# Expert stages of a two-block transformer kernel: the gate factor moves from the closing addition to the eviction of each expert's rows

## What is computed

```python
gate = (p_group * top_p / sum(top_p)).reshape(m)      # two experts a token: m = 1024 rows
x_rows = xf[row_tok].reshape(n_blocks, 128, d)        # rows sorted by expert, in blocks of 128
def expert_block(xb, e):
    hcat = xb @ w13[e]                                # 1024 -> 2 x 512
    return (silu(hcat[:, :512]) * hcat[:, 512:]) @ w2[e]
y_rows = map(expert_block, (x_rows, block_eid))
y = segment_sum(y_rows * row_gate[:, None], row_tok)  # each token: gate1 * y1 + gate2 * y2
h = layer_norm(ALPHA * h + y)
```

## Time and profile before

| | |
|---|---|
| median of 3 runs | 3498.28 us |
| lowest and highest run | 3492.36 and 3500.93 us |
| the profiled execution: its own time | 3498.12 us |
| its span in the trace | 3496.3 us |
| PE busy | 96% of the span |
| DVE, ACT, POOL busy | 71%, 54%, 9% |
| mean granted clock of PE | 0.981 of full speed |

### The profile page before, as it was taken

The page is one execution under the profiler, slowest core; times in us unless marked ns, Lnnn a source line. Parts: engine busy times, 40 slices in busy tenths (PEclk is TensorE's granted clock), DMA queues, the critical chain, the costliest instruction groups (busy, mean ns, idle before and its releaser), DMA issues.

```text
span 3496.3 us, 49987 instructions
## 1 busy us (share of the span) xinstructions
PE 3367.4 (96%) x16674; PEld 2678.1 (77%) x16674; DVE 2483.5 (71%) x3749; ACT 1879.5 (54%) x2960; POOL 326.9 (9%) x339
## 2 busy tenths in 40 slices
PE   8999999999999999999989998999999899999997
PEld 6777788887777788877778876888888676678885
DVE  7677677737676577736656457999999557579996
ACT  5566422335566422334632345888888445368885
POOL 0010000000010000000044201111111000011110
PEclk9999999999999999999999999999999999999999
DMA  4211232222111222232200007999999321189995
GB/s 166 74 48 55 73 109 97 93 98 92 65 43 61 80 103 96 97 102 76 82 19 1 19 20 282 359 365 367 355 373 387 125 73 37 49 319 371 389 379 200
DMA packets 161083, 541.89 MB, mean 155 GB/s; under 512 B 28192, under 2 KB 28192, under 8 KB 160800
## 3 DMA queue, kind: packets, MB, share of 16 engines
q1 hardware_dynamic: 141408, 510.37, 40.2%
q0 software_dynamic: 16256, 16.84, 1.5%
q10 hardware_dynamic: 3264, 12.58, 0.9%
HBM read 547.02 MB, written 34.60 MB: 166 GB/s over the span
## 4 chain that ended last, share of the span: by engine, by line
PE 84%; DVE 8%; ACT 4%; issue 2%; DMA 1%; POOL 0%; ACTq 0%; SPq 0%; POOLq 0%; DVEq 0%
PE psum L743 22%; PE psum L745 22%; PE psum L744 22%; PE psum L1085 4%; PE psum L1276 1%; PE psum L960 1%; PE psum L928 1%; DVE arena L2330 1%; PE psum L942 1%; PE psum L783 1%; PE psum L784 1%; PE psum L787 1%; DVE arena L2360 1%; PE psum L848 1%; DVE ring_rounded L2157 1%
## 5 line engine op out<-in xcount | busy, mean ns | idle before, releaser
L2880 DVE TENSOR_TENSOR ew_r<-arena,ehigh_r 128x1024 fp32r<-128x1024 f32 x648 | 750.9, 1220 | 25.2 <-ACT ehigh_r L1996 24.3
L1996 ACT ACTIVATE ehigh_r<-arena 128x1024 fp32r<-128x1024 f32 x648 | 632.3, 1052 | 36.9 <-DVE arena L2871 24.0
L1525 ACT ACTIVATE highs<-ring 128x1024 fp32r<-128x1024 f32 x282 | 298.0, 1058 | 629.6 <-PE psum L745 623.6
L2157 DVE TENSOR_TENSOR ring_rounded<-ring,highs 128x1024 fp32r<-128x1024 f32 x282 | 346.5, 1229 | 396.7 <-ACT highs L1525 396.6
L743 PE MATMUL psum<-oab_r,highs 128*128 128x512 f32 x1312 | 532.6, 406 | 5.6 <-DVE fm_r L2386 4.3
L745 PE MATMUL psum<-oab_r,ring_rounded 128*128 128x512 f32 x1328 | 525.5, 396 | 0.0
L744 PE MATMUL psum<-h_r,highs 128*128 128x512 f32 x1184 | 464.7, 392 | 0.0
L743 PE MATMUL psum<-ehigh_r,xT_high_r 128*128 128x512 f32 x864 | 352.6, 408 | 12.0 <-DVE xT_low_r L2884 6.3
L745 PE MATMUL psum<-ehigh_r,xT_low_r 128*128 128x512 f32 x864 | 341.2, 395 | 0.0
L744 PE MATMUL psum<-ew_r,xT_high_r 128*128 128x512 f32 x864 | 339.5, 393 | 0.0
L743 PEld LDWEIGHTS psum<-oab_r,highs 128*128 128x128 f32 x1312 | 247.4, 189 | 71.5 <-issue 16.6
(11 more groups left out here) (416 smaller groups left out, 6311.8 us busy)
## 6 DMA issues: line engine op xcount, KB each, us to landing
arena<-in_moe_w SPq DMA_DIRECT2D x648, 512.0 KB, 5.9
ring<-in_wstream SPq DMA_DIRECT2D x312, 512.0 KB, 3.3
arena<-rows_out_m ACTq DMA_DIRECT2D x8, 1024.0 KB, 8.0
rows_in_m<-arena ACTq DMA_DIRECT2D x4, 1024.0 KB, 4.0
x<-in_xT SPq DMA_DIRECT2D x8, 256.0 KB, 7.4
result<-x SPq DMA_DIRECT2D x8, 256.0 KB, 2.1
const<-in_const SPq DMA_DIRECT2D x1, 1112.5 KB, 10.0
arena<-rows_in_m,arena POOLq DMA_INDIRECT x58, 6.6
```

Source lines behind the costliest of these rows:

```text
L1525: act.activation(highs[:, r % HIGHS, :], ring[:, r, :], ACT.Copy) \
L1996: act.activation(ehigh_r[p], ew[:, p, :], ACT.Copy).then_inc(expert_cast[mi], 1)
L2157: dve.tensor_tensor(ring_r[:, c % R, :], ring[:, c % R, :], high.bitcast(F32), ALU.subtract).then_inc(weights_split, seq.step(ch="split"))
L2880: TT(ew_r[p], ew[:, p, :], ehigh_r[p].bitcast(F32), ALU.subtract).then_inc(expert_split[mi], 1)
```

## The change

The gates are laid out as a table by slot and job, `gate_of`, 128 by 48. At the start of the job part DVE rebuilds `job_hot`, this time multiplied by the gates; eight small matmuls on PE produce the table in PSUM bank 6; DVE copies it to SBUF between the second and the third split. Four of the eight idle products go. For every job POOL copies one column of the table to `gate_col` ahead of the scatter's own `number`, and ACT's eviction takes `gate_col` as its scale and waits for that copy. At the end of a stage DVE adds the two blocks with one addition in place of a multiplication and a multiply-add.

```diff
 def scatter(job):
+    pool.tensor_copy(gate_col, gate_of[:, bass.ds(job, 1)]).then_inc(gate_number[mi], 1)
     number(sidx, idx, job, scatter_number[mi])
     pool.wait_ge(output_out[mi], job + 2)
...
+pool.wait_ge(dve_done, seq.at(f"{m}.gate"))
 with pool.Fori(0, last) as i:
...
-idle_products(8, 7)
+pe.wait_ge(dve_done, seq.at(f"{m}.ghot"))
+for c in range(2 * NT):
+    mm = pe.matmul(psum[:, 6, 0:JOBS], place_hot[:, c, :], job_hot[:, c, :],
+                   start=(c == 0), stop=(c == 2 * NT - 1))
+mm.then_inc(pe_done, seq.step(f"{m}.gates"))
+idle_products(4, 7)
 pe.wait_ge(rows_gathered[mi], 32)
 turn_x()
...
 act.wait_ge(rows_scattered[mi], job * 16 + 16)
-act.activation(ym, psum[:, 4:6, :].rearrange("p b c -> p (b c)"), ACT.Copy) \
+act.wait_ge(gate_number[mi], job + 1)
+act.activation(ym, psum[:, 4:6, :].rearrange("p b c -> p (b c)"), ACT.Copy, scale=gate_col) \
     .then_inc(output_out[mi], 1)
...
+dve.sem_inc(settled, 1)
+step(job_hot, rows(cc("places")[:, 0:JOBS], 2 * NT), across(job, JOBS), ALU.is_equal, op=TT)
+step(job_hot, job_hot, across(rc[:, 12:14, :].rearrange("p c t -> p (c t)"), JOBS), ALU.mult, op=TT,
+     mark=f"{m}.ghot")
...
+if c == 2:
+    dve.wait_ge(pe_done, seq.at(f"{m}.gates"))
+    dve.tensor_copy(gate_of, psum[:, 6, 0:JOBS]).then_inc(dve_done, seq.step(f"{m}.gate"))
 split(c, c + 1)
...
 dve.wait_ge(rows_back[t], seq.at(f"{m}.y2{t}"))
-step(yt[:, t, :], y2[:, t, 0, :], col(12)[:, t:t + 1], None, ALU.mult, op=TS)
-dve.scalar_tensor_tensor(yt[:, t, :], y2[:, t, 1, :], col(13)[:, t:t + 1], yt[:, t, :],
-                              ALU.mult, ALU.add).then_inc(dve_done, seq.step(f"{m}.yt{t}"))
+TT(yt[:, t, :], y2[:, t, 0, :], y2[:, t, 1, :], ALU.add).then_inc(dve_done, seq.step(f"{m}.yt{t}"))
```

More of the change, by code:

```diff
@@ L228, in build @@
         (expert_used, expert_cast, expert_split, rows_turned, rows_high, rows_low, gate_silu, hidden_made,
-         hidden_turned, hidden_high, hidden_low, output_out, gather_number, scatter_number) = (
+         hidden_turned, hidden_high, hidden_low, output_out, gather_number, scatter_number, gate_number) = (
             [semaphore(f"{n}{m}") for m in range(2)]
@@ L232, in build @@
                       "gate_silu", "hidden_made", "hidden_turned", "hidden_high", "hidden_low", "output_out",
-                      "gather_number", "scatter_number"))
+                      "gather_number", "scatter_number", "gate_number"))
         psum = ctx.enter_context(nc.psum_tensor("psum", [P, 8, 512], F32))
@@ L449, in build @@
         sidx = take(1)
+        gate_col = take(1)
+        gate_of = take(JOBS)
         rnd = take(4)
```

## The result

The changed kernel takes 3509.0 us (median of 9 runs, 3506.25 to 3511.59). The kernel before, in the same session, takes 3496.25 us (9 runs, 3492.36 to 3502.72). The ratio is 1.0037, with a 95% interval of 1.0029 to 1.0045: 12.75 us slower, by 0.37%. The forecast of 3496.8 us, its range of 3491 to 3503 us and "within 0.3%" were wrong.

What follows compares the result with a forecast made beforehand. PE was taken as the bound, with 84% of the chain. 1.7 us gained at the stage ends less 0.2 us lost on evictions gave 1.5 us off 3498.28 us: 3496.8 us (rival A, chance 0.62), range 3491 to 3503 us.

Steps and rivals of the forecast that it cites:

- within 0.3%: Whole kernel: its time differs from the kernel before by no more than 0.3% (10.5 us); chance 0.91.
- 1.7 us gained, 0.2 us lost: Whole kernel: gain from the closing additions less loss from the scaled evictions after the last jobs, 1.5 us shorter.
- The sign of being wrong: Job loop: prediction is wrong if the distance between evictions differs from before by more than 0.05 us.
- Rival D: Job loop: scaled eviction (0.1 us) and a held split (0.2 us) reach PE in 54 jobs, 3513.0 us; chance 0.06.
- predicted 0.105 us: ACT's eviction: a column as scale makes it 0.105 us longer, covered in the loop by DVE's idle time.
- The end of a stage: Block additions: each 0.85 us shorter on DVE, only the last block's passes to PE, 1.7 us for two stages.
- Rival C: End of a stage: DVE sets the pace, all eight blocks gain 0.85 us, 3491.7 us; chance 0.08.
- rival E: End of a stage: PE doesn't wait for the last combination, or later waiting eats the gain, 3498.3 us; chance 0.04.
- The start of a stage: Before job 0: DVE steps and table matmuls, less four idle products, cost nothing; PE reaches its transposes 1.1 us earlier.
- Rival B: Start of m1: PE's clock falls before job 0, costing 1.4 us against 1.5 us gained, 3498.2 us; chance 0.20.
- the 1.4 us of its range: Both ends of the range: allowance for clock level changes at other places, 1.4 us both ways, taken from rival B.
- DVE's 1.06 us of idle time in a job: Job loop: DVE idle until the next SiLU, 1.06 us, taken to cover the eviction's added 0.1 us.

Runs made afterwards that it cites:

- the gates last: The changed kernel with gate_col and gate_of taken last, behind ym, so every other tile keeps its old address; 3496.47 us, ratio 0.9994 to the kernel before.
- both by 64: The kernel before with 16 unused columns ahead of ew, so PE's moving and stationary tiles both lie 64 bytes later; 3499.94 us.
- shift by 64: The kernel before with 16 unused columns behind sidx, so the tiles behind lie 64 bytes later; 3490.27 us, again in rounds 3490.97 us, ratio 0.9984.
- the last experiment: The changed kernel with gate tiles last, the other tiles 64 bytes later and the idle products placed anew; 3489.33 us, ratio 0.9978 to the kernel before.

## Why the prediction was wrong, step by step

**The step that failed** is the sentence of the sum that counted the work alone: "1.7 us gained, 0.2 us lost". It took the length of a job as given as long as no engine made PE wait, and so put PE's own time for a product at no change without a word. The two `take()` lines of the changed kernel hold no instruction, and they moved the stationary operands of 3888 products (54 x 72). The runs showed 18.106 us a job in place of 17.827 us, with the columns alone as with the whole change, and 17.827 us with all of the work at the old addresses. The term that was missing is 50 x 0.28 = 14.0 us. The sign of being wrong that the prediction named, over 0.05 us in the distance of two evictions, is the one that came.

**Rival D** named 3513.0 us and had about the right size, 0.30 us a job, by luck: its reason was another, and no idle time of PE appeared in the loop. Its conditions can be checked. An eviction takes 1.117 us in place of 1.027 us (0.09 us, predicted 0.105 us). A number copy on POOL does get longer. The timeline of a job with the change:

```profile
2383.10 5.75 DVE L2894 TENSOR_TENSOR ew_r<-arena,ehigh_r 128x1024 fp32r<-128x1024 f32 x5
...
2386.87 2.03 POOL L679 COPY arena<-arena 128x1 int32 x1 [6.87 <-PE psum L1280]
...
2390.79 0.20 POOL L691 COPY arena<-arena 128x1 f32 x1
...
2395.09 1.12 ACT L2025 ACTIVATE arena<-psum,arena 128x1024 f32<-128x1024 f32 x1 [0.43 <-PE psum L749]
```

The number copy starts inside the fourth of five splits in a row and ends with the last, after 2.03 us. The rule of the Trainium skill that stood beside the prediction (SBUF — State Buffer, section Who interferes with whom) speaks of a lock for a whole instruction; the trace agrees that such a copy is held up by a split, but it is held beyond the one that runs when it starts, through the next split too. The mean of these copies went from 575 to 1105 ns; with the columns shifted and no gate copy it is 536 ns, with the gates last 1174 ns. So the work of the change brings it (the gate copy or the longer eviction, which weren't tried apart), and the kernel with the gates last shows that it costs nothing: 17.827 us a job. The splits stay at 1217 ns. The gate copy takes 0.20 us, ends 4.1 us ahead of the eviction here, and is never its releaser.

**The end of a stage** went as predicted up to the last addition. The additions of the last blocks of `m1`, and PE's transposes behind them:

```profile
3477.16 1.22 DVE L2937 TENSOR_TENSOR arena<-arena 128x1024 f32<-128x1024 f32 x1 [15.76 <-DMA arena<-rows_out_m]
...
3479.63 1.23 DVE L2937 TENSOR_TENSOR arena<-arena 128x1024 f32<-128x1024 f32 x1 [1.24 <-DMA arena<-rows_out_m]
...
3484.70 1.22 DVE L2937 TENSOR_TENSOR arena<-arena 128x1024 f32<-128x1024 f32 x1 [1.09 <-DMA arena<-rows_out_m]
...
3485.98 0.98 PE L1356 MATMUL psum<-const,arena 128*128 128x128 f32 x7 [1.31 <-DVE arena L2937]
```

7.54 us for three steps, 2.51 us a block as in the earlier trace rows, and the idle time ahead of an addition grew from 0.3 to 1.1 us. From the first block's start to the end of the last combination it took 9.60 us before and 8.78 us with the gates last: 0.82 us in `m1` and 0.83 us in `m0`, for the 0.85 us that I gave it. Rival C, by which all blocks would gain, is out. From the first block to PE's next 128x512 products, behind the residual additions, it took 13.83 us before and 13.00 us with the change, so PE gets it and rival E is out. Not all of it stays: those products took 8.80 us at a granted clock of 0.81 before and 9.25 us at 0.76 with the change, and from the first block to the end of the kernel 0.4 us is left in this trace and 0.6 us in that of the gates-last kernel (32.98 us before, 32.60 and 32.37 us; the other kernels with the old end lie between 32.67 and 33.25 us).

**The start of a stage** was put at nothing. The way there was wrong, and the outcome was about right. The start of `m1` with the change, for the earlier trace rows:

```profile
3064.43 0.18 DVE L2881 CAST arena<-arena 128x48 int32<-128x48 f32 x1
...
3065.67 0.56 DVE L2538 TENSOR_TENSOR arena<-const,arena 128x384 f32<-128x384 f32 x1 [1.06 <-issue]
3066.26 0.56 DVE L2538 TENSOR_TENSOR arena<-arena 128x384 f32<-128x384 f32 x1
...
3066.97 3.62 PE L1307 MATMUL psum<-arena 128*128 128x48 f32 x16 [3.70 <-DVE arena L2538]
...
3070.39 5.78 PE L813 MATMUL psum<-const 128*128 128x512 f32 x8
...
3076.01 1.04 PE L1280 MATMUL psum<-const,arena 128*128 128x128 f32 x8
...
3077.08 1.02 ACT L2009 ACTIVATE xT_high_r<-psum 128x1024 fp32r<-128x1024 f32 x1 [1.96 <-PE psum L1280]
...
3079.46 0.47 PE L747 MATMUL psum<-ehigh_r,xT_high_r 128*128 128x512 f32 x1 [0.70 <-issue]
```

and a window in it (busy of PE, PEld, DVE, ACT, POOL, SP, then granted clock, DMA share, GB/s):

```profile
3069.00:3072.00 3.00, 3.00 (x10) 2.19 (x10) 1.59 (x4) 0.00 (x0) 0.00 (x0) 0.50 0.50 186
```

DVE's first step starts only 1.06 us after the cast's end, with nothing shown that it waits for. PE gets to the table matmuls 2.36 us after that end, where I had counted 1.3 us, and has been idle for 3.70 us by then. After that it works at a granted clock of 0.50, its 1.2 GHz level: the table matmuls take 3.62 us for the 1.99 us of the earlier trace rows, the four idle products 5.78 us for 4.4 us. That is what the page TensorE: Matmul & The Clock Gate of the Trainium skill, section HAM oscillation — how this bites in real kernels, says of a wait between bursts, and the trace agrees.

PE reaches its transposes 11.6 us after the cast in place of 9.0 us, and ACT now waits 1.96 us for them. From the cast to the first product it takes 15.03 us in `m1` and 14.61 us in `m0`, against 13.40 and 14.04 us before; the kernels that leave this start as it was lie between 13.2 and 14.2 us, and the one with the gates last needs 14.95 and 15.62 us.

Job 0 makes up for the late product. From the cast to the first eviction both stages together take 101.25 us before, 100.48 us with the change and 100.85 us with the gates last; the other kernels with the old start and a pace like it (both by 64, and shift by 64 twice) lie between 100.38 and 101.36 us. In `m0` the first 5 us of job 0 had a granted clock of 0.50 before and have 1.00 with the change, and from the first product to the first eviction it takes 35.32 us in place of 37.61 us. So no loss at the start is shown, and the 1.7 us of the end isn't eaten there. That the kernel with the gates last shows no gain (0.9994, 0.9985 to 1.0003) doesn't speak against it either: 1.7 us would be 0.9995, which the interval holds.

In the last experiment three idle products ahead of the wait keep PE at work. The table matmuls take 1.88 us and the transposes come 7.1 us after the cast, the first product 12.88 us in `m1` and 13.74 us in `m0`. To the first eviction both stages together take 97.75 us, where the shift by 64 bytes alone took 100.38 and 101.36 us.

**Rival B** didn't come to pass. The clock fell at the table matmuls, but was back at 1.00 for job 0 in both stages, in `m0` too, where it had been 0.50 before: the other way round than feared.

**The clock falls in another place,** for which the prediction had only the 1.4 us of its range. In the last job of a stage PE waits 2.1 to 2.3 us for `hT_low`. In 16 of the 28 stages of the 14 traces its granted clock then falls for 2.6 to 3.7 us, and the distance from the last eviction but one to the last is 9.9 to 10.1 us in place of 8.4 to 8.6 us. Here is `m1` with the gates last, whose wait was 2.25 us, and a window inside it (columns as above):

```profile
3445.09 0.49 PE L747 MATMUL psum<-ehigh_r,hT_high_r 128*128 128x512 f32 x1 [2.25 <-DVE hT_low_r L2907]
...
3447.38 0.63 PE L748 MATMUL psum<-ew_r,hT_high_r 128*128 128x512 f32 x1
...
3446.50:3449.00 2.50, 2.50 (x7) 1.97 (x6) 0.00 (x0) 0.00 (x0) 0.37 (x2) 0.50 0.26 97
```

Kernels with the old work show it in none, one or both stages, so it isn't tied to the change; why it comes in one execution and not in another stays open. It doesn't touch the distances over 31 and 19 jobs, which end before it. But it moves a whole time by about 1.5 us a stage, about as much as the gain at the end of both stages gives. The traces of the kernel before and of the changed kernel have none of it, that of the last experiment has it in both stages.

**Two readings of the prediction** were off without any weight. The rows name no releaser for DVE's 1.06 us of idle time in a job ("issue"), where the text says SiLU, and four blocks come back at the end of a stage in all, with three steps between them.

## What to carry to other kernels

A new tile in a front-to-back allocator is not free of time: it moves every tile behind it. Where PE is the bound, take new tiles behind its operands, and compare the distance from one start to the next of its matmuls with the kernel before; the idle time ahead of them shows nothing, and their mean duration only a few ns (405 to 410 ns here). If a kernel's matmuls follow one another without idle time, some padding between stationary and moving tiles is worth four or five runs; here 64 bytes gave 0.16%, and the widths that were tried lie 2.2% apart in the jobs. And a change is priced only when it has been tried with the old addresses too: its work and its layout are two changes.

## What the hardware did that I had not expected

PE's pace for products of 128x512 in fp32r goes with the distance, modulo 256 bytes, between its stationary and its moving tiles in a partition: 17.73 us for a job at a distance of 0, 18.12 us at 64 bytes. Over 72 products the step from best to worst is 0.0054 us each. It does so with DVE and ACT idle too (0.229 and 0.234 us a product in the last job). Neither side's own address does it: with the stationary tiles at one place, 17.73 and 17.81 us for two places of the moving tiles; with the moving tiles at one place, the values above for the stationary ones; and two layouts with one distance agree (18.040 and 18.042 us). No run shows what in PE or in the memory's read makes it so; that stays open. It stays open too whether other shapes and types do the same.

POOL's copy of 128 numbers can be held through the split that runs when it starts and the whole of the next, 2.03 us; a copy that falls outside of one takes 0.20 us.

PE's granted clock can fall to 0.50 after a wait of 2.1 to 2.3 us, and in other executions stays at 1.00 after the same wait: 2.21 us in the last jobs of the kernel before, where it stayed, and 2.21 us in those of the kernel with both sides moved by 64 bytes, where it fell.
